# Broadcasting gate rows to 128 partitions with TensorE products instead of DMAs through DRAM

## The reference

```python
# mLSTM: 4 heads, per head and token an input gate ig and a decay logf
logf = jax.nn.log_sigmoid(softcap(fg + f_bias))
b = jnp.cumsum(fc, axis=-1)
log_d = where(causal, b[..., :, None] - b[..., None, :] + ic[..., None, :], -inf)
s = jnp.einsum('bhtd,bhsd->bhts', qc, kc) * exp(log_d - m_t)

# attention layers, branch A: 4 heads, causal, with forget gates
c = jnp.cumsum(log_f, axis=1)
s = jnp.einsum('bqhd,bkhd->bhqk', qn, k) * scale
s = s + cqn[..., None] - c_keys
p = jax.nn.softmax(where(key_idx <= qpos, s, -inf), axis=-1)
```

## Time and profile before

| what | value |
|---|---|
| median of 3 executions | 3650.48 us (3650.34 to 3652.88) |
| the profiled execution | 3650.48 us |
| its span, first to last instruction | 3648.7 us |
| mean granted TensorE clock, as a share of 2.4 GHz | 0.981 |
| busy PE, PEld | 3466.6 us (95%), 2790.0 us (76%) |
| busy DVE, ACT, POOL | 1841.1 (50%), 776.0 (21%), 1178.4 us (32%) |

### The profile page before, as it was taken

How to read it: one execution, slowest core, us unless ns; L and a number is a source line. 1 busy time by engine, 2 the same in 40 slices (tenths; PEclk the granted TensorE clock), 3 DMA queues, 4 the chain that set the end, 5 groups by cost and what they waited for, 6 DMA issues and landing times.

```text
span 3648.7 us, 55929 instructions
## 1 busy us (share of the span) xinstructions
PE 3466.6 (95%) x22924; PEld 2790.0 (76%) x22924; DVE 1841.1 (50%) x2497; ACT 776.0 (21%) x1210; POOL 1178.4 (32%) x557
## 2 busy tenths in 40 slices
PE   5999699999999999989999999999999999999997
PEld 4888499788888888867777678888877677688886
DVE  6531566646676676753444544433534444534434
ACT  3311433211101101232222320000322232300001
POOL 2334054233344343421112223434322212244342
PEclk9999799999999999999999999999999999999998
DMA  2111000121111111121000011111310000111111
GB/s 110 53 68 46 0 4 4 51 86 47 51 46 48 50 46 52 64 94 35 24 23 29 30 72 50 46 52 46 123 41 24 29 23 24 54 62 48 50 46 64
DMA packets 40958, 174.60 MB, mean 48 GB/s; under 512 B 4576, under 2 KB 5088, under 8 KB 39536
## 3 DMA queue, kind: packets, MB, share of 16 engines
q1 hardware_dynamic: 36432, 135.85, 11.4%
q10 hardware_dynamic: 4384, 36.64, 2.7%
HBM read 157.73 MB, written 14.75 MB: 47 GB/s over the span
## 4 chain that ended last, share of the span: by engine, by line
PE 89%; DVE 7%; issue 1%; ACT 1%; DMA 1%; POOL 0%; DVEq 0%; ACTq 0%; SPq 0%; POOLq 0%
PE ps L451 53%; PE ps L887 10%; PE ps L1256 5%; PE ps L1064 3%; PE ps L1095 3%; PE ps L717 3%; PE ps L1113 3%; DVE sc L2444 1%; PE ps L1025 1%; PE ps L915 1%; PE ps L1134 1%; PE ps L1017 1%; DVE sq_sum L1813 1%; PE ps L1070 1%; PE ps L470 0%
## 5 line engine op out<-in xcount | busy, mean ns | idle before, releaser
L349 POOL TENSOR_TENSOR wH<-wraw,pv 128x1024 fp32r<-128x1024 f32 x239 | 460.0, 1925 | 2215.0 <-PE ps L451 1814.2
L451 PE MATMUL ps<-hH,wH 128*128 128x512 f32 x2800 | 882.0, 396 | 20.6 <-issue 13.3
L451 PE MATMUL ps<-hH,wL 128*128 128x512 f32 x2800 | 869.4, 392 | 0.0
L451 PE MATMUL ps<-hL,wH 128*128 128x512 f32 x2800 | 869.3, 392 | 0.0
L451 PEld LDWEIGHTS ps<-hH,wH 128*128 128x128 f32 x2800 | 522.9, 189 | 140.8 <-issue 29.6
L351 POOL TENSOR_TENSOR wL<-wraw,wH 128x1024 fp32r<-128x1024 f32 x239 | 615.3, 2574 | 18.8
L451 PEld LDWEIGHTS ps<-hL,wH 128*128 128x128 f32 x2800 | 526.1, 189 | 110.6
L451 PEld LDWEIGHTS ps<-hH,wL 128*128 128x128 f32 x2800 | 525.0, 189 | 109.2
L2259 DVE TENSOR_TENSOR xT<-ps,xT 128x512 f32<-128x512 f32 x560 | 372.2, 689 | 11.1 <-PE ps L915 11.0
L2537 DVE TENSOR_TENSOR sg<-ps,mrows 128x1024 f32<-128x1024 f32 x46 | 56.3, 1225 | 371.7 <-PE ps L451 371.7
L1694 ACT ACTIVATE sc<-sc,stat 128x256 f32<-128x256 f32 (+7 forms) x256 | 170.9, 668 | 131.8 <-DVE stat L2451 63.4
(11 more groups left out here) (388 smaller groups left out, 4295.9 us busy)
## 6 DMA issues: line engine op xcount, KB each, us to landing
wraw<-ws SPq DMA_DIRECT2D x242, 512.0 KB, 3.5
park<-xT ACTq DMA_DIRECT2D x2, 4096.0 KB, 14.0
xT<-park ACTq DMA_DIRECT2D x2, 4096.0 KB, 12.2
xT<-xin SPq DMA_DIRECT2D x1, 4096.0 KB, 12.2
xT<-xin ACTq DMA_DIRECT2D x1, 4096.0 KB, 12.2
cBs<-out ACTq DMA_DIRECT2D x8, 512.0 KB, 4.8
out<-xT SPq DMA_DIRECT2D x8, 512.0 KB, 3.5
ed<-park ACTq DMA_DIRECT2D x4, 512.0 KB, 6.6
```

Source lines behind the costliest of these rows:

```text
L349: pool.tensor_tensor(wH[:, j, :], wraw[:, j, :], zero, ALU.add).then_inc(w_hi, 1)
L451: mm = pe.matmul(pair(p)[:, half * HALF:(half + 1) * HALF], wp, hp[:, k, half * HALF:(half + 1) * HALF], start=(m == 0 and n == 0), stop=( ...
```

## The change

The rows are no longer written to DRAM and read back. PE multiplies them by a matrix of 4 rows that is one in the row of the wanted head and zero elsewhere; the product puts that row on all 128 partitions (or on 64) of a PSUM pair. In the mLSTM these are columns of the identity, broadcast (`decay_rows`, `block_decays`); for the attention, where pair i can be a register, DVE copies two columns of the identity into a new tile `select` (`gate_rows` on PE uses it). DVE's `decays` read the PSUM pair directly, `eb` and `cBs` are filled by ACT copies from PSUM. All products are f32, 4 rows deep, 512 columns wide. The functions `keep_rows`, `spread` and the ACT functions that used them go; the semaphores are renumbered. `bB_ready` now counts products, and `bB_copied` also counts ACT's copies into `cBs`.

```diff
+        select = at("select", EX3 + 4 * TILE + 2368, [P, 2, P])
...
+                def decay_rows(h):
+
+                    if h == 0:
+                        pe.wait_ge(sem("m_eb"), 2)
+                    elif h >= 2:
+                        pe.wait_ge(sem("m_dg"), h - 1)
+                    for half in range(2):
+                        mm = pe.matmul(pair(2 + h % 2)[:, half * HALF:(half + 1) * HALF],
+                                       ident[0:4, h:h + 1].to_broadcast([4, P]),
+                                       gt[0:4, 2, half * HALF:(half + 1) * HALF], start=True, stop=True)
+                    mm.then_inc(sem("bB_ready"), 1)
+
+                def block_decays(i):
+
+                    pe.wait_ge(sem("m_dg"), 3 + i)
+                    for half in range(2):
+                        for j in range(2):
+                            mm = pe.matmul(pair(2 + i)[64 * j:64 * j + 64, half * HALF:(half + 1) * HALF],
+                                           ident[0:4, 2 * i + j:2 * i + j + 1].to_broadcast([4, CH]),
+                                           gt[0:4, 3, half * HALF:(half + 1) * HALF], start=True, stop=True)
+                    mm.then_inc(sem("gate_cols"), 1)
...
                     elif i == 0:
-                        pe.wait_ge(sem("m_eb"), 2)
+                        pe.wait_ge(sem("m_eb"), 3)
...
                     pe.wait_ge(sem("m_silu"), i * 2 + 2)
-                    if i:
+                    if i == 0:
+                        pe.wait_ge(sem("m_eb"), 4)
+                    else:
                         pe.wait_ge(sem("m_ymul"), 2)
...
-                    col_gemm(*U[1], p=1, between={12: gate_columns} if i == 0 else
+                    col_gemm(*U[1], p=1, between={12: gate_columns, 18: lambda: decay_rows(0)} if i == 0 else
                              {4: lambda: normalised_tiles(0)})
                     pe.wait_ge(sem("m_raw"), i * 2 + 1)
-                    col_gemm(*U[2], p=0)
+                    col_gemm(*U[2], p=0, between={2: lambda: decay_rows(1), 10: lambda: decay_rows(2),
+                                                18: lambda: decay_rows(3)} if i == 0 else {})
                     pe.wait_ge(sem("m_raw"), i * 2 + 2)
                     pieces = {14: lambda: value_tiles(i, 0), 19: lambda: key_tiles(i)}
+                    if i == 0:
+                        pieces = pieces | {2: lambda: block_decays(0), 8: lambda: block_decays(1)}
...
+                    def gate_rows():
+
+                        pe.wait_ge(sem("fa_select"), L * 2 + i + 1)
+                        if leading:
+                            pe.wait_ge(sem("a_vtok"), L * 6 + 1)
+                        for j in range(2):
+                            for half in range(2):
+                                mm = pe.matmul(pair(2 + j)[:, half * HALF:(half + 1) * HALF], select[0:4, j, :],
+                                               fr[0:4, 1, half * HALF:(half + 1) * HALF], start=True, stop=True)
+                            mm.then_inc(sem("bB_ready"), 1)
...
-                        elif br == "B":
+                        elif br == "A":
+                            pe.wait_ge(sem("bB_copied"), L * 4 + i * 2 + 6)
+                        else:
                             pe.wait_ge(sem("a_rope"), L * 10 + i * 2 + 1)
                         value_transposes(2)
...
-                        col_gemm(*slots[3], p=1, between={2: value_tiles, 4: first_scores, 17: lambda: period(0),
+                        col_gemm(*slots[3], p=1, between={2: value_tiles, 4: first_scores, 8: gate_rows, 17: lambda: period(0),
...
-                        col_gemm(*slots[2], p=0, between={5: rotate_k} if br == "B" else {})
+                        col_gemm(*slots[2], p=0, between={5: rotate_k} if br == "B" else {16: gate_rows})
...
-            def keep_rows(dram, rows, ready, n):
-
-                act.wait_ge(sem(ready), n)
-                act.dma_start(dram, rows).then_inc(sem("rows_kept"), 16)
-
-            def spread(dst, row, kept):
-
-                act.wait_ge(sem("rows_kept"), kept * 16)
-                act.dma_start(dst, row.to_broadcast(dst.shape)).then_inc(sem("bB_ready"), 16)
...
+            def block_decays(i):
+                act.wait_ge(sem("gate_cols"), i + 2)
+                act.activation(eb[i][:, :], pair(2 + i), ACT.Copy).then_inc(sem("m_eb"), 1)
...
                 gate_logs()
-                keep_rows(park[0:4, 4, :], gt[0:4, 2, :], "gate_rows", 1)
                 raw(0, 0)
-                decay_rows()
                 block_decay_rows()
                 silu(0, 0)
                 raw(0, 1)
                 decays(0)
-                block_decays()
                 decays(1)
                 silu(0, 1)
                 decays(2)
                 channel_values(0, 0)
                 decays(3)
+                block_decays(0)
+                block_decays(1)
                 channel_values(0, 1)
...
                     if br == "A":
                         for j in range(2):
-                            spread(cBs[:, j, :], out[2 * i + j:2 * i + j + 1, L, :], L + 3)
+                            act.wait_ge(sem("bB_ready"), L * 4 + i * 2 + (5 + j))
+                            act.activation(cBs[:, j, :], pair(2 + j), ACT.Copy).then_inc(sem("bB_copied"), 1)
...
-                    dve.wait_ge(sem("bB_ready"), 64)
+                dve.wait_ge(sem("bB_ready"), h + 1)
                 for n in range(KT):
-                    ins = dve.scalar_tensor_tensor(out=ed[:, h, n * P:(n + 1) * P], in0=ed[:, h, n * P:(n + 1) * P],
+                    ins = dve.scalar_tensor_tensor(out=ed[:, h, n * P:(n + 1) * P], in0=pair(2 + h % 2)[:, n * P:(n + 1) * P],
                                                    scalar=biasT[:, 4 * n + h:4 * n + h + 1], in1=negT[:, :],
                                                    op0=ALU.add, op1=ALU.add)
...
                     keys(L, i)
+
+                    dve.tensor_copy(select[0:4, :, :], ident[0:4, bass.ds(i * 2, 2)].unsqueeze(2).to_broadcast([4, 2, P])
+                                    ).then_inc(sem("fa_select"), 1)
...
                         if br == "A" and n == 0 and j == 0:
-                            dve.wait_ge(sem("bB_ready"), 128 + (L * 2 + i + 1) * 32)
+                            dve.wait_ge(sem("bB_copied"), L * 4 + i * 2 + 6)
```

More of the change, by code:

```diff
@@ L1349, in block_decay_rows @@
                 act.activation(gt[0:4, 3, :], gt[0:4, 3, :], ACT.Exp).then_inc(sem("m_eb"), 1)
-                keep_rows(park[0:4, 5, :], gt[0:4, 3, :], "m_eb", 1)
                 act.wait_ge(sem("gate_cols"), 1)
@@ L1668, in forget_gates @@
                 act.activation(fr[0:4, 3, :], fr[0:4, 2, :], ACT.Ln, bias=1.0).then_inc(sem("gate_log"), 1)
-                keep_rows(out[0:4, L, :], fr[0:4, 1, :], "gate_rows", L + 5)
             def raw_copy(dst, p, scale=1.0):
@@ L1917, in weights @@
                                                  in1=ed[:, 2 * i + j, w], op0=ALU.mult, op1=ALU.mult).then_inc(sem("m_sd"), 1)
-                dve.wait_ge(sem("bB_ready"), 128)
+                dve.wait_ge(sem("m_eb"), 3 + i)
                 dve.scalar_tensor_tensor(out=qm[i][:, :], in0=qm[i][:, :], scalar=0.125, in1=eb[i][:, :],
```

## The result

The changed kernel takes 3693.7 us (median of 4, 3685.9 to 3696.0) beside 3651.7 for the one before (3650.3 to 3656.5): ratio 1.0109, 95% interval 1.0091 to 1.0127. It is slower, as forecast, but by 42 us and not by 22.7, and so outside the range. The profiled execution is the quickest of the changed kernel's: 3685.7 us, span 3684.0, against 3648.7 before, so 35.3 us of the loss can be read in a trace.

The account below looks back on a forecast made before the run. PE was taken as the bound, so added products cost their length: gate rows 13.8, decay rows 6.9, block decays 3.4, together 24.1, less 1.4 of stalls, gives 22.7 us on 3650.5: 3673.2 us, range 3661 to 3684.

Parts of the forecast that it names:

- The price of 0.86 us for an f32 product of 512 columns: All 32 new PE products: each costs 0.86 us, as two 128-row rotate products took 1.72 us between column-product steps.
- The stalls of 0.62 and 0.76 us before scores(1): First A pair of each attention layer: PE's standing still there goes, minus 1.4 us.
- The copies, the selects and the reordered decays: ACT copies, DVE selects and later mLSTM decays: costed at nothing, with 1.9 us cover at scores(1), 3 and 5 at block_decays.
- The 64-column products of two heads: mLSTM block_decays: eight products, two heads side by side, 3.4 us; 6.9 us without the overlap.
- The transfers in full: Rival, chance 0.03: all 25.5 us of DMA waits come off against 24.1, so 3649.1 us.
- the step that put the clock at nothing: Behind the new products in mLSTM and A pairs: granted clock stays 1.00, adding 0 us.
- the clock falls: Rival, chance 0.08: 4-row products drop the clock behind four 3.4 us insertions, 10.2 us more, so 3683.4 us.
- Half price: Rival, chance 0.13: two records of one product run together, 0.43 us per product, 12.0 us in all, so 3661.1 us.
- the forecast's two readings: Records starting together: products of rows 0 to 63 beside 64 to 127 (0.86 us each), or one product's two records (0.43).

Follow-up runs that it names:

- the last experiment: Kernel before (rows by DMA) with gate_columns after step 20 instead of 12 and ACT's channel_values(0, 0) ahead of decays(2): 3643.3 us, ratio 0.9983.

## Why the prediction was wrong

**What held.** PE is the bound, and work put into its stream costs its length. The price of 0.86 us for an f32 product of 512 columns, taken from rotate, is exact for 128 rows and 128 columns, and the sum built on it lands on the kernel with 128 rows; that it does so within 1 us is partly luck, since `block_decays` cost 0.7 us more there and other falls of the clock moved. The stalls of 0.62 and 0.76 us before scores(1) are gone, and no wait of PE for DVE or ACT came into the mLSTM stretch. The copies, the selects and the reordered decays hide. The 64-column products of two heads run side by side: eight records took 1.86 us. The transfers in full did not come back; the DMA legs of the earlier trace rows lay beside PE, as argued.

**What failed: the step that put the clock at nothing.** The sum took the granted clock behind the new products as 1.00 and gave the rival "the clock falls" 0.08. It came: windows at 0.50 behind all four `gate_rows`, the sign named for it. The rival was put aside because 3.8 us of one-column products had run at 1.00 and the product behind them too. That row doesn't speak for products of few rows: those products fill 128 rows with one column streamed, the new ones fill 4 rows with 512. The nearer row was the other one of the same group, 0.50 behind a stall and transposes of 4 rows, and the forecast explained that half clock by the stall alone. For gate_columns that is right: with the stall away, 1.15 us of the same transposes left the clock at 1.00 (the last experiment). For 1.9 us and more of 4-row products between dense ones it isn't: seven of ten such places had a fall behind them.

How much it cost: summed over windows of 2 us of the whole span, (1 - granted clock) x time is 69.8 us in the profiled execution before and 78.3 after, +8.5. Behind the four `gate_rows` 10.2 us are lost and behind three `decay_rows` 5.1; against these 15.3 stand falls of the kernel before that didn't come at their old places, or cost less: the one at gate_columns took 3.4 us before and 1.7 after. The rival named 10.2 us for the four `gate_rows`. That it is the same number is chance: it took 2.55 us for each, where two cost 1.7 and two 3.4, and it had left out the pairs.

**What was mis-sized: the price of an insertion.** The term 0.86 per product had no part for the change between the full array and a part of it. That is 0.40 us at each of the eight places of 128 columns and 0.35 at each of the two `block_decays`, 3.9 us.

The ledger of the profiled executions: 24.1 (products) - 1.4 (stalls) + 3.9 (places) + 8.5 (clock) = 35.1, measured 35.3. The same ledger for 128 rows, whose clock loss is 69.3, gives 24.1 - 1.4 + 0.7 - 0.5 = 22.9 against 21.4 of span. For 64 rows with 66.4 it gives 24.1 - 1.4 + 3.9 - 3.4 = 23.2 against 25.7, and for 32 rows with 79.6 it gives 36.4 against 33.2. So it closes within some 3 us, and the split between clock and places is no finer than that. Nor is the clock loss a property of the kernel alone, for the falls elsewhere scatter: from 140 us on the kernel before lost 64.7 us and the last experiment, with the same instructions there, 74.3.

The remaining 7 us of the median are in no trace, and their cause stays open. The quickest two executions of the changed kernel have spans of 3684.0 and 3684.1 at a mean clock of 0.979, the other three 3691.9, 3694.2 and 3691.9 at 0.976. 0.003 of 3692 us is 11, so a further loss of clock is large enough to explain it; where it fell was not seen.

**The other rivals.** Half price is refuted: the records of these products run one behind the other at 0.43 us, with 4 rows as with 128. The Trainium skill's rule (TensorE: Matmul & The Clock Gate, Part 3, "What overlaps and what doesn't"), that matmuls start and end in program order, doesn't lead to half price here. Nor does the trace of the kernel before agree with it at the products of the earlier trace rows. The last two of their records start at 418.17 and 418.19, and each raises the semaphore that the kernel lets only the last product of its half of the rows raise. So products of rows 0 to 63 ran beside those of rows 64 to 127, although the kernel issues both of the first half before the second: the first of the forecast's two readings, in which nothing helps the new products.

Two rows of the table in the section "Why this matters for your kernels" of the Trainium skill (TensorE: Matmul & The Clock Gate) bear on the rest. One gives a single product of 32 rows the same time as one of 128 rows. The pace of the records agrees, 0.43 us at either depth, but between 128-row products a pair took 2.12 us with few rows and 1.72 with 128. The other ties losses of clock in mid-kernel to gaps in which PE idles. The traces agree for gate_columns, where the fall went with the stall, and not for the 4-row products, where PE had no gap. The wait of 0.94 us some 3 us ahead of `gate_rows` in the first pairs doesn't explain the falls: the second pairs have none, and the kernels of 64 and 128 rows have the same wait without a fall.

## What to carry to other kernels

Before small-depth products go between dense ones, price them twice: their own length plus about 0.4 us for each place where they use fewer rows or columns than their neighbours, and the granted clock behind them; look in the trace for a product with the same number of rows, not for one of the same length. If few rows must be used, compare with the same product padded with zeros to 128 rows: here it bought back 21 us for four DVE operations. A broadcast by DMA whose legs lie beside a busy PE was cheaper than either, and a stall on PE's path is worth its own length and the clock behind it, once the next wait in line is taken out too.

## What the runs showed of the hardware

- The granted clock fell to 0.50 with PE busy in every window. Products of 4 rows and 128 columns led to it behind three of four pairs and all four groups of four, 32 rows behind none of the pairs and three of the groups of four, 64 and 128 rows behind none of ten places. Behind `block_decays`, 64 columns two at a time, it came at no depth. Why depth counts no run shows.
- A fall behind one insertion cost PE 1.7 or 3.4 us.
- An f32 product of 512 columns took 0.86 us with 128 rows. With 4 or 64 rows a pair took 2.12 us instead of 1.72, and a single one of 4 rows 1.26; the weights of the first product behind each change of rows, or to 64 columns, were not loaded ahead.
- Products on rows 0 to 63 and on rows 64 to 127 ran side by side, and so did products of 64 columns of two heads.
- Products of 4 rows and 8 columns weren't free either: a pair cost PE 0.74 us and a group of four 1.19.
